# Two transformer blocks on one core: modulation blocks 0 to 10 summed in PE column groups, attention's divisions on DVE, value products one pair later, other load order

## The chip, the core and the metric

The kernel runs on one NeuronCore of a Trainium2 chip. Five engines work from queues of their own, in program order: PE (TensorE, matmuls), DVE (VectorE), ACT (ScalarE), POOL (GpSimd) and SP (SyncE, which here only issues DMAs). They wait for one another through semaphores that the program sets by hand. The metric is the device time of one execution in microseconds; lower is better. The median of three runs before the change is 988.04 us.

## What is computed

The input is a sequence of 256 tokens of width 1024. It goes through two blocks of a transformer, then through a third of another kind and a last norm. All weights are fp32.

```python
def first_block(x, c, ...):
    cond = silu(c)
    for i in range(2):
        mod = cond @ ada_w[i] + ada_b[i]                  # 1024 -> 6 * 1024
        sh1, sc1, g1, sh2, sc2, g2 = split(mod, 6)
        h = rmsnorm(x, norm1_g[i]) * (1 + sc1) + sh1
        y = sliding_window_sink_attention(h) if i == 0 else stick_breaking_attention(h)
        x = x + g1 * y
        h = rmsnorm(x, norm2_g[i]) * (1 + sc2) + sh2
        x = x + g2 * swiglu(h, w_gate[i], w_up[i], w_down[i])
    return x

def sliding_window_sink_attention(h):                     # 16 query heads of 64, 2 key heads
    ...                                                   # softmax over window and one sink column
    p = softmax(concat([s, sink])) [..., :-1]
    o = p @ v
    return o @ w_o
```

The third block takes its own `c_2` and `ada_w_2`. Its mixer is a spatial gate beside a causal convolution with a group norm, then an output projection `w_out` over both normed halves and a gated feed-forward of the same size. A last norm is shifted and scaled by `c_2 @ ada_f_w`.

The modulation vectors are 40 blocks of 512 outputs: blocks 0 to 11 are the first layer's, 12 to 23 the second's, 24 to 39 those of the third block and the last norm. Each block reads 1024 x 512 weights (2 MB).

## The kernel before

The activations lie transposed, [128 partitions, 8 tiles, 256 tokens]. Each weight matrix is streamed in units of 128 x 2048 fp32 (1 MB) into RAW, which has four slots. `high` on ACT rounds a unit to WH (fp32r), `low` on DVE takes the rest WL = RAW - WH, and PE makes three products for each tile (`three`: high by high, high by low, low by high; the lines 1739, 1740 and 1741 of the trace). A slot is loaded anew when its `low` is done (`unit_free`).

The modulation blocks are streamed through ADA, a buffer of one block with two halves; the first four blocks have places of their own (ADA, RAW twice, ADA3). `ada_sum` on DVE makes the product: eight instructions over [128, 512], each adding a weight tile times a column of COND to ACC (lines 1091 and 1094). For blocks 0 to 9 `ada_reduce` on PE then sums over the partitions, with four one-column matmuls, into AUX, and DVE adds the bias (`early_bias`, `ada_bias`) into MOD. Of block 3 the first four tiles go through PE alone (`ada_direct`). From block 10 on DVE transposes ACC in 32 x 32 blocks and sums, and four blocks are folded in one PE step (`fold_reduce`, line 1848).

The start: SP loads blocks 0 to 3 and x, and then the first projection's weights. PE turns x, ACT norms it. With MOD of blocks 0 to 3, `coefficients(0)` gives the scale (line 1153), ACT and DVE write the high and low parts of the scaled rows, and PE starts the key and value products.

The attention works on eight pairs of query heads, b = 0 to 7. For each, PE makes the scores (`sa_scores`), DVE the maxima (`sa_max`, lines 1448 to 1467), ACT the exponentials with their sums (`sa_exp`, lines 854 and 859), DVE the sum's reciprocal (`sa_divide`, lines 1475 and 1477), ACT the divisions (its own `sa_divide`, line 866), PE turns the weights (`sa_turn`, line 2099), ACT copies them (line 877), PE multiplies with the values (`sa_rows`, lines 2109 to 2113), ACT takes the high part (line 883) and DVE the low (`attn_low`, line 1483). The order is written out by hand, with scores, maxima and exponentials two pairs ahead; half a modulation block is summed on DVE in each pair.

From the second norm on, every norm starts in `first_group`: PE multiplies with unscaled rows UH and UL while the norm's root is still being made. ACT writes a row's high part and its square (lines 684 and 685), DVE the low part (`unscaled_low`, line 1168, whose operands X and UH lie in SBUF). The squares of tiles 0 to 3 are added on POOL (`square_sum`, lines 627 and 631, both operands in SBUF), and PE sums the others and that sum over the partitions (`norm_sums`, line 1894), between the second and the third row of the group. Norms 2 and 4 follow a feed-forward (`add_down`), norms 1, 3 and 5 an output projection (`add_out`), norm 6 is the last.

In the third block's output projection PE takes the groups' sums (`group_sums`), the group roots (`group_spread`), the sums of the second half's norm (`out_norm(1)`) and its root (`out_spread(1)`) between the tiles of units 0 and 1; unit 2 needs the rows normed with them, whose low parts are DVE's line 1690.

## Time and profile before

| | us |
|---|---|
| three runs, median (lowest to highest) | 988.04 (986.56 to 990.71) |
| the profiled execution, its own time | 988.17 |
| its span in the profile | 986.4 |
| PE busy | 940.4 (95%) |
| DVE busy | 797.1 (81%) |
| ACT busy | 496.2 (50%) |
| POOL busy | 34.0 (3%) |

The span is what the profile covers, from the first to the last instruction; the execution's own time is 1.8 us longer. PE is busy nearly throughout from 139 us to the end; before that it is not. The view by stretches tells, for each stretch, the busy time of each engine and the granted clock of PE (1.00 is 2.4 GHz, 0.50 is 1.2 GHz). In the timeline a row is a start, a duration, the engine, line, operation and tiles, a count of merged instructions and, in brackets, how long the engine had been idle and who released it. An fp32 matmul stands there as two records.

### The profile page before, as it was taken

Reading aid. Unit: us, or ns where it says so; the run is one execution under the profiler, and the core shown is the slowest. Engines: PE = TensorE matmul, PEld = TensorE weight load, DVE = VectorE, ACT = ScalarE, POOL = GpSimd, SP = SyncE. Lnnn points to the kernel's source line nnn. Section 1 sums busy time; section 2 is a strip of 40 time slices with the busy share of each in tenths; the row PEclk is TensorE's granted clock in tenths of the full one; section 3 lists DMA queues with packets and bytes.
Section 4 is the critical chain, followed back from the end, with each engine's and each line's share of the span. In section 5 each row is a group of like instructions: output and inputs, shape, how many; then the busy total and the mean of one; then the engine's idle time right before and its main releaser. Section 6 shows DMA issues by size and latency. Waiting matters only on the chain.

```text
span 986.4 us, 19404 instructions
## 1 busy us (share of the span) xinstructions
PE 940.4 (95%) x7627; PEld 900.5 (91%) x7627; DVE 797.1 (81%) x1155; ACT 496.2 (50%) x754; POOL 34.0 (3%) x52
## 2 busy tenths in 40 slices
PE   1898889999999999999999999999999999999998
PEld 1796569999999999988999999999988999999997
DVE  6885986999859989787699995999995599985832
ACT  2734955554433367565655443336665555443432
POOL 0400000000000010000000000003000000000001
PEclk9797869999999999999999999999999999999999
DMA  9990586499929997565159992998784349992911
GB/s 319 375 338 36 163 263 226 159 323 317 320 74 373 372 339 258 206 223 183 45 164 309 320 323 79 366 373 272 257 211 147 112 154 304 332 311 93 368 58 64
DMA packets 147473, 234.99 MB, mean 238 GB/s; under 512 B 6746, under 2 KB 78082, under 8 KB 147410
## 3 DMA queue, kind: packets, MB, share of 16 engines
q1 hardware_dynamic: 145328, 230.88, 68.4%
q0 software_dynamic: 1408, 2.62, 1.0%
q10 hardware_dynamic: 674, 0.63, 0.3%
q8 instruction: 42, 0.69, 0.3%
q14 instruction: 21, 0.17, 0.0%
HBM read 230.79 MB, written 1.05 MB: 235 GB/s over the span
## 4 chain that ended last, share of the span: by engine, by line
PE 81%; DVE 10%; DMA 3%; issue 2%; SPq 1%; ACT 1%; DVEq 0%; ACTq 0%
PE M L1739 20%; PE M L1740 19%; PE M L1741 19%; DVE ACC L1094 5%; DMA ADA<-in_ada_w 3%; PE AUX L1894 2%; DVE WL L1068 2%; PE M L1757 1%; PE M L1759 1%; PE M L1763 1%; PE AUX L2327 1%; PE AUX L1806 1%; PE AUX L1807 1%; PE M L1811 1%; PE AUX L1811 1%
## 5 line engine op out<-in xcount | busy, mean ns | idle before, releaser
L1739 PE MATMUL M<-XH,WH 128*128 128x256 f32 x1264 | 363.2, 287 | 4.8 <-DVE XL L1690 2.2
L664 ACT ACTIVATE WH<-RAW 128x2048 fp32r<-128x2048 f32 x135 | 257.1, 1913 | 219.7 <-DMA RAW<-in_w_down 69.9
L1740 PE MATMUL M<-XL,WH 128*128 128x256 f32 x1264 | 359.3, 284 | 0.0
L1741 PE MATMUL M<-XH,WL 128*128 128x256 f32 x1264 | 359.2, 284 | 0.0
L1068 DVE TENSOR_TENSOR WL<-RAW,WH 128x2048 fp32r<-128x2048 f32 x135 | 307.4, 2285 | 40.1 <-ACT WH L664 39.8
L1739 PEld LDWEIGHTS M<-XH,WH 128*128 128x128 f32 x1264 | 244.4, 193 | 7.2 <-issue 6.6
L1740 PEld LDWEIGHTS M<-XL,WH 128*128 128x128 f32 x1264 | 244.4, 193 | 0.3
L1741 PEld LDWEIGHTS M<-XH,WL 128*128 128x128 f32 x1264 | 244.2, 193 | 0.0
L1094 DVE SCALAR_TENSOR_TENSOR ACC<-ADA,COND,ACC 128x512 f32<-128x512 f32 x262 | 196.8, 751 | 9.1 <-DMA ADA<-in_ada_w 0.2
L1739 PE MATMUL M<-MH,WH 128*128 (+1 forms) x528 | 150.6, 285 | 1.3 <-DVE WL L1068 0.6
L1740 PE MATMUL M<-ML,WH 128*128 (+1 forms) x528 | 149.4, 283 | 0.0
L1741 PE MATMUL M<-MH,WL 128*128 (+1 forms) x528 | 149.4, 283 | 0.0
L1739 PEld LDWEIGHTS M<-MH,WH 128*128 128x128 f32 x528 | 101.2, 192 | 3.2 <-issue 3.1
L1740 PEld LDWEIGHTS M<-ML,WH 128*128 128x128 f32 x528 | 101.3, 192 | 0.0
L1741 PEld LDWEIGHTS M<-MH,WL 128*128 128x128 f32 x528 | 101.3, 192 | 0.0
L713 ACT ACTIVATE MH<-TMP 128x256 f32 (+1 forms) x66 | 25.1, 417 | 54.1 <-DVE TMP L1214 46.7
L1139 DVE SCALAR_TENSOR_TENSOR X<-M,MOD,X 128x256 f32<-128x256 f32 x48 | 20.5, 477 | 16.3 <-PE M L1741 16.3
L1858 PEld LDWEIGHTS AUX<-CONST,ACC 128*128 128x128 f32 x72 | 11.6, 246 | 23.0 <-DVE ACC L1094 23.0
L1858 PE MATMUL AUX<-CONST,ACC 128*128 128x1 f32 x72 | 12.1, 289 | 21.3 <-DVE ACC L1094 21.3
L627 POOL TENSOR_TENSOR SQS<-TMP 128x256 f32<-128x256 f32 x6 | 4.7, 781 | 723.0 <-ACT TMP L685 720.9
L1127 DVE TENSOR_TENSOR MOD<-AUX,VC 128x16 f32<-128x16 f32 (+1 forms) x8 | 1.4, 172 | 34.5 <-PE AUX L1848 34.5
L707 ACT ACTIVATE TMP<-M 128x256 f32<-128x256 f32 x60 | 19.3, 373 | 18.1 <-PE M L1741 18.1
(321 smaller groups left out, 1312.2 us busy)
## 6 DMA issues: line engine op xcount, KB each, us to landing
ADA<-in_ada_w SPq DMA_DIRECT2D x68, 1024.0 KB, 5.6
RAW<-in_w_gate SPq DMA_DIRECT2D x44, 512.0 KB, 6.1
RAW<-in_w_up SPq DMA_DIRECT2D x44, 512.0 KB, 7.4
RAW<-in_w_down SPq DMA_DIRECT2D x44, 512.0 KB, 8.0
RAW<-in_w_ffn_in SPq DMA_DIRECT2D x44, 512.0 KB, 6.8
RAW<-in_wqkv_b SPq DMA_DIRECT2D x24, 512.0 KB, 5.0
RAW<-in_w_ffn_out SPq DMA_DIRECT2D x22, 512.0 KB, 6.7
RAW<-in_w_in SPq DMA_DIRECT2D x16, 512.0 KB, 6.6
```

The source lines that it names most:

```text
L664: act.activation(WH[:, s, :], RAW[:, s, :], ACT.Copy).then_inc(h_ready, 1)
L707: act.activation(TMP[:, 2 * g + n, :], M[:, 4 * g + n, :], ACT.Silu).then_inc(silu_ready, 1)
L713: act.activation(MHF[:, bass.ds((i * 4 + 2 * g + n) * T, T)], TMP[:, 4 + 2 * g + n, :], ACT.Copy).then_inc(midh_ready, 1)
L1068: dve.tensor_tensor(WL[:, s, :], RAW[:, s, :], WH[:, s, :], ALU.subtract).then_inc(l_ready, 1)
L1094: dve.scalar_tensor_tensor(out=acc, in0=w, scalar=scale, in1=acc, op0=ALU.mult, op1=ALU.add).then_inc(a_chain, 1)
L1139: dve.scalar_tensor_tensor(out=X[:, j, :], in0=M[:, j, :], scalar=mod(layer, chunk, j), in1=X[:, j, :], op0=ALU.mult, op1=ALU.add).then_in ...
L1739: pe.matmul(out_ap, wh, xh, start=start, stop=False, skip_group_check=True)
L1740: pe.matmul(out_ap, wh, xl, start=False, stop=False, skip_group_check=True)
L1741: return pe.matmul(out_ap, wl, xh, start=False, stop=stop, skip_group_check=True)
L1811: mm = pe.matmul(FIRST[m], WH[:, s, cols], UL[:, kt, :], start=False, stop=kt == KT - 1, skip_group_check=True)
L1858: mm = pe.matmul(AUX[:, 6, at + j:at + j + 1], ACC[:, acc_slot(b), j * P:(j + 1) * P], cc(C_ONE), start=True, stop=True)
L1894: mm = pe.matmul(sums[:, n * m:n * m + n], squares[:, m * P:(m + 1) * P], columns, start=first and m == 0, stop=last, skip_group_check=True)
```

## The change

- Modulation blocks 0 to 10 are no longer summed on DVE. `ada_rows` on PE multiplies each weight tile, as the moving operand of 512 columns, with a column of COND that is broadcast to 32 columns; tile kt goes to column group kt mod 4, so that the four groups write four partial sums to the 32-partition bands of SUMS (AUX 6 and 7). `ada_turn` on DVE transposes SUMS and copies 16 columns into PART, and the blocks are folded as the later ones are: 0 to 3, 4 to 7, 8 and 9, then 10 to 13 and so on.
- On PE the blocks stand at the start, after units 2 and 3 of the first projection, before the first scores, after the second, and in pairs 1, 3 and 5.
- The divisions of the attention are four DVE instructions right behind the reciprocal. In a pair PE makes the scores first, then turns the weights, and multiplies the values of the pair before; ACT and DVE take the high and low part a pair later too.
- Loads: the rows of c go through ACT's queue; the larger part of the constants is loaded after the first rounding of the key and value weights; the loads of `wo_a` alternate with those of modulation blocks 5 to 8, and the loads of blocks up to 11 wait for PE's sums and not for DVE's.
- Norms: POOL adds the squares of five tiles instead of four, and PE has one less to sum.
- Output projection of the third block: ACT squares the centred rows straight from AUX, before `high` of unit 3, and DVE copies them after that; `group_sums` and `group_spread` stand one tile earlier, `out_norm(1)` after the first tile of unit 1 instead of the third, and `out_spread(1)` before its last tile.

On PE, one pair of the attention before (pair 2: weights turned, scores of pair 4, a reduction, value products; PR holds the softmax weights, PT the turned ones, VA the values):

```order
L2099 MATMUL AUX<-CONST,PR 128x128 x6
L2085 MATMUL M<-KS,QA 128x128
L2085 MATMUL M<-QA 128x128
L2087 MATMUL M<-KS,QA 128x256
L2087 MATMUL M<-QA 128x256
L2089 MATMUL M<-MASKA,IDB 128x384 x2
L1858 MATMUL AUX<-CONST,ACC 128x1 x4
L2109 MATMUL AUX<-PT,VA 64x128 x2
L2111 MATMUL AUX<-PT,VA 64x128 x2
L2113 MATMUL AUX<-PT,VA 64x128 x2
```

And after, pair 3, which carries a whole modulation block (line 1853):

```order
L2067 MATMUL M<-KS,QA 128x128
L2067 MATMUL M<-QA 128x128
L2069 MATMUL M<-KS,QA 128x256
L2069 MATMUL M<-QA 128x256
L2071 MATMUL M<-MASKA,IDB 128x384 x2
L2081 MATMUL AUX<-CONST,PR 128x128 x6
L2091 MATMUL AUX<-PT,VA 64x128 x2
L2093 MATMUL AUX<-PT,VA 64x128 x2
L2095 MATMUL AUX<-PT,VA 64x128 x2
L1853 MATMUL AUX<-ADA,COND 32x512 x8
```

The scores moved ahead of the turning, and eight matmuls over 512 columns took the place of four of one column.

On DVE, one pair of the attention before (reciprocal, maxima, half a block's sum, low part):

```order
L1475 TENSOR_TENSOR SM<-RS_SUM,SM 128x4
L1477 RECIPROCAL SM<-SM 128x4
L1448 TENSOR_REDUCE SM<-M 128x2 x2
L1462 TENSOR_TENSOR SM<-SM,QRS 128x4
L1464 SCALAR_TENSOR_TENSOR SM<-SM,NSINK 128x4
L1467 TENSOR_TENSOR SM<-SINK,SM 128x4
L1120 TENSOR_TENSOR MOD<-AUX,VC 128x4
L1091 TENSOR_SCALAR ACC<-ADA,COND 128x512
L1094 SCALAR_TENSOR_TENSOR ACC<-ADA,COND,ACC 128x512 x3
L1483 TENSOR_TENSOR XL<-AUX,XH 128x256
```

And after, in pair 3, from the reciprocal on:

```order
L1459 RECIPROCAL SM<-SM 128x4
L1463 TENSOR_SCALAR PR<-PR,SM 128x128
L1463 TENSOR_SCALAR PR<-PR,SM 128x256
L1463 TENSOR_SCALAR PR<-PR,SM 128x128
L1463 TENSOR_SCALAR PR<-PR,SM 128x256
L1432 TENSOR_REDUCE SM<-M 128x2 x2
L1446 TENSOR_TENSOR SM<-SM,QRS 128x4
L1448 SCALAR_TENSOR_TENSOR SM<-SM,NSINK 128x4
L1451 TENSOR_TENSOR SM<-SINK,SM 128x4
L1470 TENSOR_TENSOR XL<-AUX,XH 128x256
L1104 STREAM_TRANSPOSE ACC<-AUX 128x512
L1106 COPY PART<-ACC 128x16
```

The four divisions now stand between the reciprocal and the maxima of the next pair, and the half block's sum is gone, with a transpose and a copy in three of the eight pairs.

The diff, cut to its core:

```diff
-FOLDED = 10
-FOLDS = [range(b, min(b + 4, 40)) for b in range(FOLDED, 40, 4)]
+ON_PE = 11
+EARLY_FOLDS = [range(0, 4), range(4, 8), range(8, 10)]
+FOLDS = EARLY_FOLDS + [range(b, min(b + 4, 40)) for b in range(10, 40, 4)]
...
                     if b == len(EARLY):
-                        sp.wait_ge(a_chain, 4 * h + 4)
+                        sp.wait_ge(a_rows, h + 1)
+                    elif b <= ON_PE:
+                        sp.wait_ge(a_rows, 2 * (b - 1) + h + 1)
                     else:
                         sp.wait_ge(a_chain, summed(b - 1, 4 * h + 4) + 8 * i)
                     sp.dma_start(ADA[:, h, :, :], src[:, 4 * h:4 * h + 4, bass.ds(col, 512)]).then_inc(a_landed[h], 16)
...
-            for k in range(3):
+            for k in range(4):
                 load_square(U0["wo_a"], k, wo_a_src, 512 * (k // 2))
-            ada_block(5)
-            load_square(U0["wo_a"], 3, wo_a_src, 512)
-            for b in range(6, 11):
+                ada_block(5 + k)
+            for b in range(9, 11):
                 ada_block(b)
...
-                for j in range(2, 4):
+                for j in range(2, 5):
                     pool.wait_ge(sq_ready, KT * n + j + 1)
-                    pool.wait_ge(sq_sum, 3 * (n - 1) + j - 1)
+                    pool.wait_ge(sq_sum, 4 * (n - 1) + j - 1)
                     pool.tensor_tensor(SQS[:, :], SQS[:, :], TMP[:, j, :], ALU.add).then_inc(sq_sum, 1)
...
+            act.dma_start(CONST[:, KEPT_EARLY:K_W], a["kept"][:, KEPT_EARLY:K_W]).then_inc(rest_in, 16)
...
-            def sa_divide(b):
-                act.wait_ge(sa_r, b + 1)
-                p = b % 2
-                for e in range(2):
-                    for blk, lo, hi in ((0, 0, P), (1, P, 3 * P)):
-                        act.activation(PR[:, p, e, lo:hi], PR[:, p, e, lo:hi], ACT.Copy,
-                                       scale=SM[:, p, 5, 2 * e + blk:2 * e + blk + 1]).then_inc(sa_pn, 1)
+            def attn_high(b):
+                act.wait_ge(sa_o, b + 1)
+                act.activation(XH[:, b, :], AUX[:, 4, :], ACT.Copy).then_inc(hh_ready, 1)
             sa_exp(0)
-            sa_divide(0)
...
-                if b + 1 < 8:
-                    sa_divide(b + 1)
+                if b > 0:
+                    attn_high(b - 1)
                 if b + 2 < 8:
                     sa_exp(b + 2)
-                act.wait_ge(sa_o, b + 1)
-                act.activation(XH[:, b, :], AUX[:, 4, :], ACT.Copy).then_inc(hh_ready, 1)
+            attn_high(7)
...
+            for j in range(4):
+                act.wait_ge(gn_c, j // 2 + 1)
+                act.activation(TMP[:, j, :], AUX[:, j, :], ACT.Square).then_inc(gn_sq, 1)
             high(U0["w_out"], 3)
-            for j in range(4):
-                act.wait_ge(gn_copied, j + 1)
-                act.activation(TMP[:, j, :], CV[:, j, :], ACT.Square).then_inc(gn_sq, 1)
             act.wait_ge(gn_var, 1)
...
+            def ada_turn(b):
+                turned = ACC[:, b % 2, :]
+                if b >= 2:
+                    dve.wait_ge(part_ready, b - 1)
+                dve.wait_ge(a_rows, 2 * b + 2)
+                dve.transpose(turned, SUMS).then_inc(acc_turned, 1)
+                dve.wait_ge(acc_turned, b + 1)
+                dve.tensor_copy(PART[:, part_at(b):part_at(b) + 16], turned.rearrange("p (x r) -> p x r", r=32)[:, :, 0]).then_inc(part_ready, 1)
...
+            ada_turn(0)
             dve.wait_ge(ang_s, 2)
             dve.tensor_scalar(COS[:, :], COS[:, :], cc(C_ROPE), cc(C_KEEP), ALU.mult, ALU.add).then_inc(trig_ready, 1)
-            ada_sum(3, 0, rows=range(4, 8))
+            ada_turn(1)
+            root(0)
+            ada_turn(2)
+            ada_turn(3)
...
+            fold_bias(0)
+            coefficients(0)
             kv_low(0, kv_high, kv_low_ready)
-            early_bias()
-            coefficients(0)
             dve.wait_ge(t_ready, KT)
             dve.wait_ge(coef_ready, 1)
...
-                    dve.wait_ge(sa_pn, 4 * b - 4)
                 dve.tensor_tensor(SM[:, p, 4, :], RS_SUM[:, p, :], SM[:, p, 3, :], ALU.add).then_inc(sa_t, 1)
                 dve.wait_ge(sa_t, b + 1)
                 dve.reciprocal(SM[:, p, 5, :], SM[:, p, 4, :]).then_inc(sa_r, 1)
+                dve.wait_ge(sa_r, b + 1)
+                for e in range(2):
+                    for blk, lo, hi in ((0, 0, P), (1, P, 3 * P)):
+                        dve.tensor_scalar(PR[:, p, e, lo:hi], PR[:, p, e, lo:hi], SM[:, p, 5, 2 * e + blk:2 * e + blk + 1], None,
+                                          ALU.mult).then_inc(sa_pn, 1)
...
             qa_group(2)
+            ada_turn(6)
             sa_divide(0)
             sa_max(1)
+            ada_turn(7)
             for b in range(8):
                 if b + 1 < 8:
                     sa_divide(b + 1)
...
                     qa_recip(2)
                 if b + 2 < 8:
                     sa_max(b + 2)
-                if b % 2 == 0 and b > 0:
-                    ada_bias(5 + b // 2)
-                half = KT // 2 * (b % 2)
-                ada_sum(6 + b // 2, 0, rows=range(half, half + KT // 2))
-                attn_low(1, b)
-            low(U0["wo_a"], 1)
-            ada_bias(9)
-            low(U0["wo_a"], 2)
-            ada_sum(10, 0)
-            low(U0["wo_a"], 3)
+                if b > 0:
+                    attn_low(1, b - 1)
+                if b in (0, 4):
+                    fold_bias(1 + b // 4)
+                elif b in (1, 3, 5):
+                    ada_turn(8 + b // 2)
+            attn_low(1, 7)
+            for k in range(1, 4):
+                low(U0["wo_a"], k)
             add_out("wo_a", 0, 0)
...
-            def ada_reduce(b):
-                pe.wait_ge(a_chain, summed(b, KT))
-                if b > 3:
-                    pe.wait_ge(mod_ready, b)
-                at = 4 * b if b < 3 else 0
-                for j in range(4):
-                    mm = pe.matmul(AUX[:, 6, at + j:at + j + 1], ACC[:, acc_slot(b), j * P:(j + 1) * P], cc(C_ONE), start=True, stop=True)
-                mm.then_inc(acc_red, 1)
+            def ada_rows(b, h):
+                if b < len(EARLY):
+                    pe.wait_ge(early_landed[b][h], 16)
+                else:
+                    pe.wait_ge(a_landed[h], 16 * (b + 1 - len(EARLY)))
+                if h == 0 and b > 0:
+                    pe.wait_ge(acc_turned, b)
+                    if b in [fold[0] for fold in FOLDS]:
+                        pe.wait_ge(mod_ready, b)
+                w = EARLY[b if b < len(EARLY) else 0]
+                for kt in range(4 * h, 4 * h + 4):
+                    c = slice(32 * (kt % 4), 32 * (kt % 4) + 32)
+                    mm = pe.matmul(SUMS[c, :], COND[:, kt:kt + 1].to_broadcast([P, 32]), w[:, kt, :], start=h == 0, stop=h == 1,
+                                   skip_group_check=True)
+                mm.then_inc(a_rows, 1)
...
             def norm_sums(n):
-                for j in range(4, 6):
-                    mean_square(n, j)
-                pe.wait_ge(sq_sum, 3 * n)
+                mean_square(n, 5)
+                pe.wait_ge(sq_sum, 4 * n)
                 token_means(AUX[:, 0, 0:2], SQS, ONES[:, 0:1], False, False)
...
-            ada_reduce(0)
+            pe.wait_ge(cond_ready, 1)
+            ada_block(0)
+            pe.wait_ge(early_rows_in, 16 * row_dmas(EARLY_ROWS))
+            turn_rows(EARLY_ROWS)
+            ada_block(1)
             pe.wait_ge(x_in, 16)
             for j in range(KT):
                 for m in range(2):
                     mm = pe.transpose(M[:, j, m * P:(m + 1) * P], XTOK[:, m, j * P:(j + 1) * P], IDENT)
                 if j % 2 == 1:
                     mm.then_inc(x_turned, 1)
-            ada_reduce(1)
...
+            ada_rows(2, 1)
+            ada_block(3)
+            fold_reduce(0)
...
+            ada_block(7)
             for b in range(8):
-                sa_turn(b)
                 if b + 2 < 8:
                     sa_scores(b + 2)
-                if b % 2 == 0 and b > 0:
-                    ada_reduce(5 + b // 2)
-                sa_rows(b)
-            ada_reduce(9)
+                sa_turn(b)
+                if b > 0:
+                    sa_rows(b - 1)
+                if b in (0, 4):
+                    fold_reduce(1 + b // 4)
+                elif b in (1, 3, 5):
+                    ada_block(8 + b // 2)
+            sa_rows(7)
             group(U0["wo_a"], 0, 0, 0, 1)
...
-            unit(base, 0, 0, sets[0], range(0, 4), operand, True, False, between=[lambda: None, group_sums, group_spread])
+            unit(base, 0, 0, sets[0], range(0, 4), operand, True, False, between=[group_sums, group_spread, lambda: None])
             pe.wait_ge(ug_ready, 4)
-            unit(base, 1, 0, sets[1], range(0, 4), operand, True, False, between=[lambda: None, lambda: None, lambda: out_norm(1)])
-            out_spread(1)
+            unit(base, 1, 0, sets[1], range(0, 4), operand, True, False, between=[lambda: out_norm(1), lambda: None, lambda: out_spread(1)])
...
-            mean_square(6, 4)
             for j in range(4):
                 last_turn(j)
             mean_square(6, 5)
```

## Rows read from the trace of the kernel before

**Rows 1.** The page: the span.

```profile
span 986.4 us, 19404 instructions
```

**Rows 2.** By stretches: PE, PEld, DVE, ACT, POOL busy us, granted clock, DMA.

```profile
95.00:139.00 44.00, 34.59 (x234) 23.32 (x234) 37.45 (x94) 36.91 (x121) 0.00 (x0) 0.73 0.52 169
...
190.00:430.00 240.00, 239.44 (x1959) 233.87 (x1958) 210.29 (x264) 117.34 (x145) 4.10 (x3) 1.00 0.80 278
...
770.00:774.00 4.00, 3.63 (x18) 3.66 (x19) 1.23 (x4) 3.98 (x4) 0.00 (x0) 0.57 0.02 4
```

**Rows 3.** Timeline of the start, DVE and PE: start, duration, instruction, idle before.

```profile
32.78 0.48 DVE L1091 TENSOR_SCALAR ACC<-ADA,COND 128x512 f32<-128x512 f32 x1 [1.77 <-DMA ADA<-in_ada_w]
...
38.67 0.16 DVE L1114 TENSOR_TENSOR MOD<-AUX,VC 128x4 f32<-128x4 f32 x1 [1.16 <-PE AUX L2001]
...
40.40 0.55 PE L1739 MATMUL M<-XH,WH 128*128 128x256 f32 x1 [1.77 <-DVE XL L1366]
```

**Rows 4.** Prices: page group, timeline of PE's column groups, lines' durations (ns).

```profile
L1094 DVE SCALAR_TENSOR_TENSOR ACC<-ADA,COND,ACC 128x512 f32<-128x512 f32 x262 | 196.8, 751 | 9.1 <-DMA ADA<-in_ada_w 0.2
...
734.98 5.39 PE L2327 MATMUL AUX<-ADA,DG 128*32 128x256 f32 x96
...
L1103 DVE STREAM_TRANSPOSE ACC<-ACC x30: 711/712/715, 149.4 to 921.3; 128x512 f32<-128x512 f32 x30
```

**Rows 5.** Timeline of the attention: ACT, DVE and PE, pairs 0 to 7.

```profile
92.03 0.46 ACT L854 ACTIVATE PR<-M,SM,QRS 128x128 f32<-128x128 f32 x1
...
104.25 0.15 DVE L1475 TENSOR_TENSOR SM<-RS_SUM,SM 128x4 f32<-128x4 f32 x1
...
104.64 1.49 ACT L866 ACTIVATE PR<-PR,SM 128x128 f32<-128x128 f32 x4 [0.37 <-DVE SM L1477]
104.66 0.95 DVE L1448 TENSOR_REDUCE SM<-M 128x2 f32<-128x256 f32 x2
...
106.05 0.46 ACT L854 ACTIVATE PR<-M,SM,QRS 128x128 f32<-128x128 f32 x1
...
108.02 0.20 ACT L859 ACTIVATE SM<-SM 128x4 f32<-128x4 f32 x1
...
126.38 0.44 ACT L854 ACTIVATE PR<-M,SM,QRS 128x128 f32<-128x128 f32 x1
...
129.55 1.87 PE L1858 MATMUL AUX<-CONST,ACC 128*128 128x1 f32 x8 [2.47 <-DVE ACC L1094]
...
137.79 1.87 PE L1858 MATMUL AUX<-CONST,ACC 128*128 128x1 f32 x8 [1.21 <-DVE ACC L1094]
```

**Rows 6.** Timeline: a DVE scaling of 256 columns by a column of scales.

```profile
7.37 0.35 DVE L1329 TENSOR_SCALAR ANG<-ANG,CONST 128x256 f32<-128x256 f32 x1
```

**Rows 7.** Timeline of the third block's output projection, PE.

```profile
767.59 0.60 PE L1902 MATMUL AUX<-CONST,RSTD 128*128 128x128 f32 x4
...
770.37 0.55 PE L1739 MATMUL M<-XH,WH 128*128 128x256 f32 x1 [2.17 <-DVE XL L1690]
```

**Rows 8.** Timeline of norm 2: DVE, POOL and PE.

```profile
362.06 1.27 DVE L1168 SCALAR_TENSOR_TENSOR UL<-X,COEF,UH 128x256 fp32r<-128x256 f32 x3
362.10 1.82 POOL L631 TENSOR_TENSOR SQS<-SQS,TMP 128x256 f32<-128x256 f32 x1
363.36 0.84 DVE L1168 SCALAR_TENSOR_TENSOR UL<-X,COEF,UH 128x256 fp32r<-128x256 f32 x1
364.12 2.28 DVE L1068 TENSOR_TENSOR WL<-RAW,WH 128x2048 fp32r<-128x2048 f32 x1
364.22 0.58 PE L1894 MATMUL AUX<-CONST,SQS 128*128 128x1 f32 x4
```

**Rows 9.** Timeline of norm 3: POOL, DVE and PE.

```profile
487.95 0.74 POOL L631 TENSOR_TENSOR SQS<-SQS,TMP 128x256 f32<-128x256 f32 x1
488.80 0.47 DVE L1168 SCALAR_TENSOR_TENSOR UL<-X,COEF,UH 128x256 fp32r<-128x256 f32 x1
490.34 0.58 PE L1894 MATMUL AUX<-CONST,SQS 128*128 128x1 f32 x4
```

151 lines of the change are left out of this document (56 added, 95 removed).

## The prediction, made before the changed kernel was run

> **What bounds the kernel now.** I read the page's span first [rows 1], then the view by stretches, in order of time [rows 2]. From 190 to 430 us PE is busy 239.4 of 240 us at full clock, and it stays so nearly to the end: there every microsecond of PE's work, and every wait of PE, goes straight into the time, and work taken off DVE brings nothing. Between 95 and 139 us, in the attention, it is otherwise: DVE is busy 37.5 of 44 us, ACT 36.9, PE 34.6 at a mean clock of 0.73. So the change's large edit, modulation off DVE, can pay only before 139 us, by letting PE reach the output projection earlier; behind that only edits of PE's own row count. The timelines of single stretches follow: the start [rows 3], the attention [rows 5], the one long wait of PE in the third block [rows 7], and the norms [rows 8, 9]. The sum is made against the profiled execution's own 988.17 us, its span and 1.8 us around it; the median of the runs, 988.04, is the same within 0.2.
>
> **The price of a block on PE.** DVE pays eight instructions of 0.75 us for a block, 6.0 us [rows 4], and PE a reduction of 1.87 at half clock [rows 5], about 1.0 at full. For the new form the nearest row is the convolution, which runs 128x32 matmuls in four column groups: 96 records in 5.39 us [rows 4] are 12 sets of four fp32 matmuls of 256 columns, 0.45 us a set, so the four groups do run side by side. At 512 columns a set is 0.9, a block 1.8 us; at half clock 3.6. DVE then has a transpose of 0.71 [rows 4] and a small copy, 0.9 together. PE pays more than before, DVE 5 us less a block.
>
> **The start.** The last weights of block 3 land at 32.78, the first modulation is added up at 38.67, and PE starts at 40.40 [rows 3]. After: half a block 0.9 to 1.8, transpose and copy 0.9, the fold some 0.5, bias 0.2, so 2.5 to 3.4 us behind the landing instead of 5.9. The landing comes up to 1.7 us earlier (SP begins without two issues; a third of a megabyte of constants follows later). But the first `low` of the key weights, 1.1 us, now stands behind the coefficients. That gives 2 to 4.5 us at the first product. Until the first exponential PE then pays 0.75 to 1.0 more for each of blocks 4 and 5 and 1.8 for block 6. I take a first exponential 1.4 us earlier, bounds 0 to 3.
>
> **The attention.** Before, the first exponential starts at 92.03 and the eighth at 126.38, 4.9 us a pair [rows 5]. What paces it after? The exponentials of a pair take 108.22 - 106.05 = 2.2 us; then DVE adds and inverts (104.25 to 104.64, 0.4), and from 104.66 to 106.05 it makes the next pair's maxima, 1.4 [rows 5]. The divisions, 1.49 on ACT [rows 5], today run beside these maxima. On DVE they stand ahead of them: two of 256 columns at 0.27 apart (0.35 less overlap, [rows 6]) and two of 128 at 0.20 to 0.27, 0.9 to 1.1 us. The new ring is 2.2 + 0.1 + 0.4 + 1.0 + 1.4 = 5.0 us: exponentials, reciprocal, divisions, the next maxima, the next exponentials. It has taken the place of the old pace: ACT and DVE get idle time and the pair stays at 5 us. Seven pairs are 35.0 instead of 34.35, a loss of 0.7. The order on PE (scores first) keeps this ring free of PE for about 3 us of delay: PE was busy 34.6 us for eight pairs at a clock of 0.73 [rows 2], 4.3 a pair, which is some 3.2 at full clock and 6 at half; a block adds 1.8 or 3.6. At full clock that is less than the ring or level with it, at half clock more; I allow 1.3 us for stretches at half clock.
>
> The end of the attention is shorter. Before, PE waited 2.47 us for a DVE sum and reduced it for 1.87 ahead of pair 6's value products, and again 1.21 and 1.87 ahead of the projection [rows 5]. Both go. The second is 3.1 us on the path whole; of the first I count 1.4, since the turning of the last weights is next behind it. Value products a pair later cost nothing there: the last pair's products wait for the low part of the pair before as they do now. Together 4.5. The attention and what is before it: 1.4 - 0.7 - 1.3 + 4.5 = **3.9 us** earlier at the projection, bounds 0 to 7. The `high` and `low` of `wo_a` unit 1 follow the attention by 4.6 us and lie under unit 0, which PE works on for 5.8 us or more; the first gate weights now load before it, since SP no longer stands behind block 9's sum. Behind 139 us PE is full, so the 3.9 us stay.
>
> **The third block's output projection.** PE waits 2.17 us for the normed rows, which come 2.8 us after the root was spread at 767.59 [rows 7], and then has a mean clock of 0.57 for 4 us [rows 2]: some 3.3 us at 1.2 GHz, which costs 1.5. After: squares before `high`, sums one tile earlier, `out_norm(1)` two tiles earlier and the spread ahead of the last tile, some 2.3 us earlier in PE's own work. About 0.7 us of wait is left, after which the trace shows no fall of the clock. Gain 1.5 + 1.4 = **2.9 us**, bounds 1 to 3.6.
>
> **The norms.** One square less on PE is 0.4 us in each of six norms, if POOL's added tile is there in time. In norms 1 and 6 it is (in norm 1 DVE idles then; in norm 6 its other operand is in PSUM): 0.8. In norm 2 it is not. POOL's last add began at 362.10, just after DVE's first `unscaled_low`, and took 1.82 us instead of the 0.74 of norm 3 [rows 8, 9]: it came through only where DVE had a gap, before the instruction at 363.36, which in turn took 0.84 instead of 0.48. It ended at 363.92, and PE took the sum at 364.22 [rows 8]. So a POOL add waits while DVE runs instructions with two SBUF operands back to back. The fifth tile's add would start at 364.06, while the last `unscaled_low` ends and `low` follows at 364.12 without a gap, also with two SBUF operands (RAW and WH), until 366.3. I take it that POOL waits for that too: its add ends at 367.05, PE takes the sum at 367.1, 2.9 us later than today, with some 3 us idle. After 2.17 us of idling the clock cost 1.5 us above; I put 1.6 here. Norm 4's records lie the same. Cost 2 x (2.9 + 1.6) = **9.0 us**; lower bound, if POOL gets in at 364.06, 0.7 a norm. The Trainium skill, page SBUF — State Buffer, section Who interferes with whom, has the rule: a DVE instruction with two SBUF inputs contends with a GpSimd one that reads SBUF, and whoever is first holds the shared port for the whole instruction. The trace agrees for the `unscaled_low` (1.82 against 0.74); for `low` no row shows it.
>
> In norms 3 and 5 POOL's fifth add would start at 488.83, within 0.03 us of a DVE instruction at 488.80 [rows 9] that is followed by three more and a `low`. It could go first (gain 0.4), slip in before the fourth, or wait to 492.6. I take nothing for both, between +0.4 gained and 3.2 lost each.
>
> **Sum.** 988.2 - 3.9 - 2.9 - 0.8 + 9.0 = 989.6 us: the gains are eaten by one moved addition.
>
> **Rivals.**
> R1, POOL gets in: it takes its turn ahead of `low`, and each of norms 2 and 4 costs 0.7 while 3 and 5 give 0.4 each: 988.2 - 3.9 - 2.9 - 0.8 - 0.8 + 1.4 = 981.2. For it: the start is only 0.06 us from DVE's, and a pending instruction may be served between two others. Against it: in the run of three that starts at 362.06 it was not, at two boundaries [rows 8].
> R2, POOL is shut out in all four norms: norms 3 and 5 cost 3.2 + 1.6 each, since `low` there follows the four at 0.4 apart, from 490.4 to 492.6, and PE's sum is today at 490.34 [rows 9]: 999.2. It is on the slower side, and decides at whether POOL or DVE asks first at 488.8.
> R3, PE paces the attention: if it stays at half clock (0.73 was the mean, [rows 2]) a pair needs 6 us and one with a block 9, and the gain of 3.9 turns into 0 to 3 lost: 995 with the norms as forecast, 987 with R1. Against it: PE will idle less.
> R4, the column groups don't overlap for 512 columns (four times the price, 5.4 us more for each of eleven blocks): over 1020; the convolution speaks against it.
>
> **How the numbers follow.** Forecast 0.40 (987 to 993), R1 0.32 (978 to 984), R2 0.13, R3 0.11, others 0.04. The range leaves out the low edge of R1 and the high edge of R2: 979 to 998. A measurement can tell 0.5% here, 4.9 us: faster than 983.1 is most of R1 and little of the forecast, 0.31; slower than 993 is R2, most of R3 and the upper edge of the forecast, 0.30; the rest 0.39.
>
> **What would show it.** In the profile after: sums of a block of about 0.9 us a half on PE; exponentials 5.0 us apart; the first product of the output projection near 135.6; POOL's fifth add of norms 2 and 4 lasting some 3 us, with a PE idle of about 3 us before the sum of POOL's squares and a lower clock behind it; the wait of unit 2 of `w_out` under 1 us. I am wrong if POOL's fifth add takes 0.74 us there, or if the exponentials come every 4 us.

## The result and the profile after

The changed kernel takes 979.58 us in the median (978.55 to 981.21, four runs), the kernel before 989.38 on the same chip (986.56 to 993.56). The ratio is 0.990, with a 95% interval of 0.987 to 0.993. The kernel before scatters by some 10 us from run to run (984.1 to 994.3 over all runs below), so kernels from different chips are compared by their ratios only, and differences of 2 us or less are read in the traces. The prediction was wrong: it forecast 989.6 us, no gain at all, and the time lies 10 us below that, at the lowest edge of its whole range (979 to 998). The time is near that of rival R1 (981.2), but, as the next sections show, by another sum.

The page of the profiled execution (its own time is 978.55), span and first section:

```profile
span 976.8 us, 19474 instructions
PE 937.0 (96%) x7691; PEld 878.8 (90%) x7691; DVE 756.9 (77%) x1118; ACT 484.8 (50%) x722; POOL 39.4 (4%) x58
```

DVE has lost 40 us of work and the span 9.6 us [rows 1]. By stretches (busy us of PE, PEld, DVE, ACT and POOL, granted clock, DMA share, GB/s):

```profile
96.00:128.00 32.00, 23.85 (x235) 13.42 (x233) 22.28 (x85) 20.51 (x75) 0.00 (x0) 1.00 0.63 217
131.50:150.00 18.50, 18.50 (x142) 18.50 (x141) 11.06 (x10) 12.62 (x13) 0.00 (x0) 0.90 0.73 241
190.00:430.00 240.00, 238.64 (x1926) 231.75 (x1925) 208.03 (x261) 118.55 (x150) 4.82 (x4) 0.99 0.79 276
```

The same stretch of the attention in the kernel before:

```profile
96.00:128.00 32.00, 26.59 (x190) 16.43 (x188) 27.84 (x77) 29.10 (x103) 0.00 (x0) 0.81 0.49 157
```

From 96 us on, in the attention's loop, PE now runs at full clock where it had 0.81 (the 0.73 of [rows 2] takes in the start and the end of the attention, which are at half clock in both kernels), and has 8 of 32 us free. From 190 to 430 us, where it was always busy at full clock before [rows 2], it now idles for 1.4 us and the clock falls once. The timeline of PE at the start and in the attention (start, duration, instruction, idle before it and who ended that):

```profile
33.15 0.26 PE L1837 MATMUL AUX<-PART,CONST 128*32 128x16 f32 x8 [1.16 <-DVE PART L1106]
36.22 0.47 PE L1727 MATMUL M<-XH,WH 128*128 128x256 f32 x1 [2.81 <-DVE XL L1353]
...
109.93 1.92 PE L1853 MATMUL AUX<-ADA,COND 128*32 128x512 f32 x16
...
131.50 0.58 PE L1745 MATMUL M<-XH,WH 128*128 128x256 f32 x1
```

and the projection's first product in the kernel before:

```profile
139.52 0.56 PE L1757 MATMUL M<-XH,WH 128*128 128x256 f32 x1
```

ACT and DVE around pair 3, and ACT's first and last exponentials:

```profile
88.24 0.46 ACT L858 ACTIVATE PR<-M,SM,QRS 128x128 f32<-128x128 f32 x1
...
98.36 0.46 ACT L858 ACTIVATE PR<-M,SM,QRS 128x128 f32<-128x128 f32 x1 [1.24 <-DVE SM L1448]
...
100.63 0.16 DVE L1457 TENSOR_TENSOR SM<-RS_SUM,SM 128x4 f32<-128x4 f32 x1 [2.02 <-ACT SM L863]
100.83 0.18 DVE L1459 RECIPROCAL SM<-SM 128x4 f32<-128x4 f32 x1
101.04 1.01 DVE L1463 TENSOR_SCALAR PR<-PR,SM 128x128 f32<-128x128 f32 x4
...
102.13 0.95 DVE L1432 TENSOR_REDUCE SM<-M 128x2 f32<-128x256 f32 x2
...
103.51 0.46 ACT L858 ACTIVATE PR<-M,SM,QRS 128x128 f32<-128x128 f32 x1 [1.95 <-DVE SM L1448]
...
123.74 0.46 ACT L858 ACTIVATE PR<-M,SM,QRS 128x128 f32<-128x128 f32 x1 [1.85 <-DVE SM L1448]
```

The first product is at 36.22 (40.40 before [rows 3]), the first exponential at 88.24 (92.03 [rows 5]), the projection's first product at 131.50, where it was at 139.52. These are single traces, and the starts scatter: two more traces of the changed kernel (a_again, a_again_b, below) have the projection at 133.30 and 132.43, two more with the start of the kernel before (b_pool_five, b_out_between) at 141.59 and 143.03. The means of the three are 132.4 and 141.4, 9.0 us apart. A whole block costs PE 1.92 us at full clock (estimate: 1.8). From pair 3 on ACT waits 1.85 to 1.95 us in each pair for DVE, which goes through reciprocal, divisions and maxima one behind the other. Norm 2, one of the two norms in which the prediction put its 9 us (POOL, DVE, PE; the groups of [rows 8]):

```profile
352.50 1.81 POOL L633 TENSOR_TENSOR SQS<-SQS,TMP 128x256 f32<-128x256 f32 x1
353.76 0.83 DVE L1156 SCALAR_TENSOR_TENSOR UL<-X,COEF,UH 128x256 fp32r<-128x256 f32 x1
354.45 0.73 POOL L633 TENSOR_TENSOR SQS<-SQS,TMP 128x256 f32<-128x256 f32 x1
354.52 2.81 DVE L1067 TENSOR_TENSOR WL<-RAW,WH 128x2048 fp32r<-128x2048 f32 x1
355.24 0.61 PE L1886 MATMUL AUX<-CONST,SQS 128*128 128x1 f32 x4 [0.93 <-POOL SQS L633]
```

POOL's added addition starts 0.07 us ahead of `low`, takes 0.73 us, and it is `low` that pays: 2.81 instead of 2.28 us [rows 8]. PE waits 0.93 us. In the output projection of the third block, the waits of PE from 755 to 768 us (engine, what waited and for whom: us, times, longest):

```profile
PE M L1727 <- DVE XL L1678: 0.7, 1, 0.7
```

The wait of 0.7 us was 2.17 before [rows 7]. Put together, by the start of POOL's first addition in each norm (159.01, 359.53, 486.18, 681.02, 782.96 and 975.13 us before; 150.00, 349.93, 478.79, 673.54, 773.27 and 965.93 after):

| stretch | forecast | measured |
|---|---|---|
| to the output projection | -3.9 | -8.0 |
| projection to norm 1 | 0 | -1.0 |
| norm 1 to 2 | -0.4 | -0.6 |
| norm 2 to 3 | +4.5 | +2.2 |
| norm 3 to 4 | 0 | -0.1 |
| norm 4 to 5 (with `w_out`) | +1.6 | -2.2 |
| norm 5 to 6 | 0 | +0.5 |
| norm 6 to the end | -0.4 | -0.4 |
| sum | +1.4 | -9.6 |

Two questions follow: what POOL's addition costs and why, and what in the attention gives 8 us.

### The profile page after: what moved, and what is told of

Its sections match the earlier page's. It is cut to its first block, busy times and chain, and to the rows that moved or that the text cites. A ratio compares the mean times of both kernels' runs of the same rounds, so it can differ in the third digit from the quotient of the medians.

```text
span 976.8 us, 19474 instructions
## 1 busy us (share of the span) xinstructions
PE 937.0 (96%) x7691; PEld 878.8 (90%) x7691; DVE 756.9 (77%) x1118; ACT 484.8 (50%) x722; POOL 39.4 (4%) x58
## 4 chain that ended last, share of the span: by engine, by line
PE 83%; DVE 8%; ACT 3%; DMA 2%; issue 2%; POOL 1%; SPq 0%; DVEq 0%; ACTq 0%; POOLq 0%
PE M L1727 21%; PE M L1728 20%; PE M L1729 20%; DVE WL L1067 2%; DMA TMP<-in_x 2%; PE AUX L1886 2%; PE AUX L1853 1%; PE M L1745 1%; PE M L1747 1%; PE M L1751 1%; PE AUX L2314 1%; ACT PR L858 1%; POOL SQS L633 1%; PE AUX L1794 1%; PE AUX L1799 1%
## 5 line engine op out<-in xcount | busy, mean ns | idle before, releaser
L1727 PE MATMUL M<-XH,WH 128*128 128x256 f32 x1264 | 361.9, 286 | 3.8 <-DVE XL L1353 2.8
L1084 DVE SCALAR_TENSOR_TENSOR ACC<-ADA,COND,ACC 128x512 f32<-128x512 f32 x203 | 152.5, 751 | 7.0 <-DMA ADA<-in_ada_f_w 0.3
L1745 PE MATMUL M<-XH,WH 128*128 128x256 f32 x96 | 25.3, 294 | 0.0
L1211 DVE TENSOR_TENSOR ML<-TMP,MH 128x256 f32 (+1 forms) x66 | 24.8, 418 | 0.5 <-ACT MH L717 0.5
```

The lines of the kernel that those rows point to most:

```text
L1084: dve.scalar_tensor_tensor(out=acc, in0=w, scalar=scale, in1=acc, op0=ALU.mult, op1=ALU.add).then_inc(a_chain, 1)
L1211: dve.tensor_tensor(MLF[:, at], TMP[:, 4 + 2 * g + n, :], MHF[:, at], ALU.subtract).then_inc(mid_ready, 1)
L1727: pe.matmul(out_ap, wh, xh, start=start, stop=False, skip_group_check=True)
L1745: pe.matmul(M[:, tau, :], WH[:, s, cols], xh, start=first and q == 0 and tau % 2 == 0, stop=False, skip_group_check=True)
```

## Experiments on GpSimd's addition and the clock

The first theory A was that the addition is worth little where it is in time and costs where it is late; the prediction had said that it is shut out by `low`. A and B are named anew in each expectation.

**Taken back.** In all norms, and then in norms 2 and 4 alone:

```diff
-                for j in range(2, 5):
+                for j in range(2, 4):
```

> The changed kernel with GpSimd's fifth square addition taken back in all six norms (three tiles added up behind the first pair's, PE takes four squares itself again). Theory A (the late addition costs in norms 2 and 4, where PE waited 0.93 us for it and the granted clock then fell to 0.67 for 4 us, and gives about 0.1 us of PE time in the others): no wait of PE for GpSimd's sum in norm 2, clock 1.00 behind it, the stretch from norm 2 to norm 3 back from 128.9 to 126.7 us; in all 1.5 to 3 us faster than the changed kernel, 976.5 to 978. Theory B (the addition is worth its 0.4 us of PE in every norm, and the lost clock behind norm 2 is chance): 2 us slower, 981.5, and the stretch from norm 2 to norm 3 stays at 128.5 or more.

Measured: 976.32 us, ratio 0.9885 (0.9867 to 0.9903), an interval that overlaps with that of the changed kernel (0.987 to 0.993). From norm 2 to 3 it takes 126.64 us, and PE has no wait there: theory A in this stretch. But two falls of the clock now stand behind norms 1 and 5 (201.80 and 193.51 us to the next norm, instead of 199.93 and 192.66), and of the 4.5 us saved behind norms 2 and 4 one or two are left.

```diff
-                for j in range(2, 5):
+                for j in range(2, 5 if n not in (2, 4) else 4):
```

> The changed kernel with the fifth addition taken back in norms 2 and 4 alone. Theory A: as with all six taken back in norms 2 and 4, and 0.1 to 0.4 us kept in each of norms 1 and 6: 976 to 977.5. Theory B: 0.8 us slower than the changed kernel, 980.4.

Measured: 978.84, ratio 0.9913 (0.9897 to 0.993): nearer to theory B, though again inside the interval of the changed kernel. PE does not wait in norm 2, and the clock fell all the same; the 8 us that begin 4 us behind the norm's start, and one of them alone:

```profile
355.18:363.18 8.00, 8.00 (x58) 8.00 (x57) 4.81 (x8) 3.85 (x7) 0.38 (x1) 0.79 0.85 300
358.00:359.00 1.00, 1.00 (x7) 1.00 (x6) 0.12 (x2) 0.00 (x0) 0.00 (x0) 0.50 0.61 227
```

PE was busy all 8 us, at a mean clock of 0.79 and for a time at 0.50, and the way to norm 3 took 128.31 us. So a fall needs no wait of PE; theory A's cause of the falls was too simple.

**Alone in the kernel before.** The same line the other way round, 4 to 5.

> The kernel before with GpSimd's fifth square addition alone. Theory A (the addition gets in ahead of the long subtraction, in 0.7 to 1.0 us; PE waits some 0.9 us for it in norms 2 and 4 and saves 0.4 in norms 1 and 6): within 1.5 us of before, 986 to 988.5. Theory B, my prediction (the addition is shut out until the subtraction is over): 3 us for that addition in norms 2 and 4, 8 to 9 us slower, 996. Theory C (0.4 us saved in every norm): 985.

Measured: 989.39 against 989.04, ratio 1.0001 (0.9977 to 1.0026). Theory A. The added addition costs nothing that can be measured (the interval is some 2.5 us to either side), where the prediction had it at 8.2 (9.0 less 0.8).

**The changed kernel again.**

> The changed kernel itself, once more, beside the others of this group. The question is where the granted clock falls behind 150 us, each fall costing some 1.7 us: in the first trace in norms 2 and 4. Theory A (the wait of 0.93 us for GpSimd's sum brings the fall): the same two norms again, and nowhere else before the tail. Theory B (any norm's run of one-column matmuls may bring it, and which one does so is chance): at least one fall in another norm, or a different number of them; the wait of 0.93 us stays where it was. Time 977 to 979.5 either way, since two falls are usual in all traces so far.

Measured: 979.54, ratio 0.9897 (0.984 to 0.9953), and the falls stand behind norms 2 and 4 again. That looks like theory A, but over all traces of this document the falls are a matter of counts. From norm 2 to norm 3 the kernels with a wait of 0.9 us took 128.86 to 128.95 us in eight traces and 130.41 in one, with a fall each, and 127.29 and 127.30 in two, without one. The kernels without the wait took 126.64 to 126.66 in five traces and 128.31 in one, with the fall shown above. So **the wait itself costs 0.65 us and a fall 1.6**, and a fall came in nine of eleven traces with the wait and in one of six without. Kernels without the additions had falls behind norm 1 or 5 instead, in four of five traces.

**One addition more.** Whether `low` holds POOL at all was open, since the fifth tile's addition came ahead of it in every trace. With a sixth tile one comes due behind `low`:

```diff
-                for j in range(2, 5):
+                for j in range(2, 6):
```

> The changed kernel with one more tile of squares on GpSimd (a sixth), so that an addition comes due in norms 2 and 4 while the vector engine's long subtraction stands ready to start or runs. Theory A (the two engines take turns: whichever is asked first runs its whole instruction, and the other goes next, so the subtraction starts 0.5 us late behind the fifth addition and the sixth then waits for its whole 2.3 us): sixth addition over at about 358.4 in a trace whose norm 2 starts at 349.9, PE waits 3.5 to 4.3 us there, 5 to 7 us slower than the changed kernel. Theory B (an addition is never held for long by the subtraction, the fifth was not at its start only by luck): sixth addition 0.7 to 1.0 us, PE waits 1.7 us, 1 to 2 us slower.

Measured: 988.1 us, ratio 1.0002 (0.998 to 1.0025), 8.5 us slower than the changed kernel of the same chip (979.61). Theory A, and somewhat dearer. POOL and DVE in norm 2:

```profile
355.92 0.73 POOL L633 TENSOR_TENSOR SQS<-SQS,TMP 128x256 f32<-128x256 f32 x1
355.99 2.81 DVE L1067 TENSOR_TENSOR WL<-RAW,WH 128x2048 fp32r<-128x2048 f32 x1
356.79 2.59 POOL L633 TENSOR_TENSOR SQS<-SQS,TMP 128x256 f32<-128x256 f32 x1
```

and the wait of PE there, from 351 to 361 us:

```profile
PE AUX L1886 <- POOL SQS L633: 3.7, 1, 3.7
```

The fifth addition comes first and `low` waits for it; the sixth asks 0.8 us behind `low`'s start and is held until `low` ends at 358.80, then takes its 0.6. Norm 2 to norm 3 took 132.45 us. This is what the prediction had described for the fifth: the mechanism exists and was put one addition too early. The Trainium skill, page SBUF — State Buffer, section Who interferes with whom, calls the port pair that DVE and GpSimd share an exclusive lock and says that the order of issue decides who blocks. The trace agrees in both directions (2.81 instead of 2.28 us for DVE, 2.59 instead of 0.73 for POOL).

## Experiments on the attention and the start

**The modulation and its load order alone.** Divisions on ACT, products in the same pair with PE's old order, four tiles on POOL, `w_out` as before (the edits below, together):

> The changed kernel with all but the modulation blocks and the load order undone: divisions on ScalarE, value products in the same pair and PE's order of the pair as before, four tiles on GpSimd, the output projection as before. Theory A (nearly all of the gain ahead of the output projection is the modulation: no wait of PE for the vector engine's sums at the start, in the units and at the two ends of the attention, and a vector engine free of 3 us a pair): first exponential near 88.3, projection at 131 to 133, 978 to 981.5. Theory B (the later value products and the divisions carry the attention's part, the modulation gives only the 3.8 us of the start): projection at 135 to 136.5, 983 to 984.5.

Measured: 975.35 us, ratio 0.987 (0.9806 to 0.9935), better than either theory said and at least as good as the whole change (979.54 on this chip; the intervals overlap). First exponential 88.42, projection 129.53. The modulation on PE, with its load order, carries the gain; the rest of the change adds nothing to it that can be measured. No run takes these two apart. The load order may have a share at the start: SP issues the first load of block 3 at 11.06 us, where it was 14.28, and the products of block 3 at 30.06 wait for DVE's transpose of the block before and no longer for a DMA.

**The divisions.** ACT's `sa_divide` put back, its call after the copies of each pair:

```diff
+            def sa_divide(b):
+                act.wait_ge(sa_r, b + 1)
+                p = b % 2
+                for e in range(2):
+                    for blk, lo, hi in ((0, 0, P), (1, P, 3 * P)):
+                        act.activation(PR[:, p, e, lo:hi], PR[:, p, e, lo:hi], ACT.Copy,
+                                       scale=SM[:, p, 5, 2 * e + blk:2 * e + blk + 1]).then_inc(sa_pn, 1)
```

> The changed kernel with attention's divisions back on ScalarE, where they run beside the vector engine's maxima. Theory A (ring): 2.2 + 0.4 + 1.5 + 0.2 = 4.2 to 4.5 us a pair instead of 5.06, so 4 to 6 us earlier at the projection, 974 to 976: moving the divisions was a loss. Theory B (the divisions on ScalarE hold up its copies and exponentials, as in the kernel before, where a pair took 4.9): 4.8 to 5.1 us a pair and 978.5 to 980.5.

Measured: exponentials 4.45 us apart (88.86 to 120.01), as the ring says, projection at 129.26; the time of 977.5 (0.9893, 0.9868 to 0.9917), which lies between the ranges of the two theories, did not show it, since behind norm 2 a longer fall of the clock made it 130.41 us to norm 3. Once more on one chip with its rivals:

> The changed kernel once more, as the measure for the two that follow on the same chip. Falls of the clock behind 150 us: by theory A of its first repetition in norms 2 and 4 again. 0.99 of the time of before.

Measured: 979.61, ratio 0.9915 (0.9888 to 0.9943). In norm 4 POOL's additions were shorter this time (3.00 us the three, instead of 4.26) and PE waited only 0.2 us for them (norm 4 to 5: 97.34 us), as also in two further traces (a_max_first and a_ring_double, 3.01 and 3.02 us); behind norm 2 the clock fell again. The expectation held at norm 2 alone.

> Divisions back on ScalarE, once more beside the changed kernel on one chip, with more rounds. Theory A (the shorter ring, 4.45 against 5.06 us in the traces, is worth the 2 to 3 us that the projection is earlier): 2 to 3.5 us faster than the changed kernel of this group. Theory B (behind the attention the clock takes it back, as the first medians suggest): within 1 us.

Measured: 974.58, ratio 0.9864 (0.9838 to 0.989), 5 us faster than the changed kernel beside it. Theory A in direction, and more than its 2 to 3.5; the two traced executions are 2.3 apart (span 973.7 against 976.0), since neither is the median of its kernel (975.49 and 977.77 us). The pairs were 4.45 apart but for one of 5.8. **Moving the divisions to DVE was a loss**: some 2 us at the projection in the traces, 0.5 and 5 us in the two comparisons of times.

**The order on DVE.** In the loop over the pairs:

```diff
-                if b + 1 < 8:
-                    sa_divide(b + 1)
                 if b == 1:
                     qa_recip(2)
                 if b + 2 < 8:
                     sa_max(b + 2)
+                if b + 1 < 8:
+                    sa_divide(b + 1)
```

> The changed kernel with the maxima of a pair issued on the vector engine ahead of the reciprocal and divisions of the pair before it. Theory A (the pace of 5.06 us a pair is a ring: exponentials 2.2, reciprocal 0.4, divisions 1.0, maxima 1.4, each behind the other; with the maxima running beside the exponentials it opens, and the next limit is PE with some 3.2 us a pair and 1.9 for a block): exponentials 3.8 to 4.4 us apart, the first product of the output projection 5 to 7 us earlier, 973 to 975. Theory B (PE, its scores and its blocks, paces the attention, and the ring only seems to fit): exponentials stay within 0.3 us of 5.06, and the time within 1 us of the changed kernel.

Measured: 971.13, ratio 0.9835 (0.9816 to 0.9854). The pairs come 4.28 us apart (90.79 to 120.78) and the projection at 128.35. Theory A by the pace; the time is 2 us better than its range, the projection 3.2 us earlier and not 5 to 7, since in this trace the first exponential was 2.5 us later. The waits between 96 and 128 us name what may limit next, the turned weights, the blocks' DMA and PE:

```profile
ACT PT L877 <- PE AUX L2081: 5.8, 5, 2.4
PEld AUX L1853 <- DMA ADA<-in_ada_w: 4.9, 3, 2.1
DVE ACC L1104 <- PE AUX L1853: 3.6, 4, 1.4
PEld M L2067 <- ACT PR L858: 3.3, 3, 1.6
ACT PR L858 <- DVE SM L1448: 3.2, 2, 2.9
```

In the changed kernel the wait of the exponentials for the maxima was the largest, from 99 to 128 us:

```profile
ACT PR L858 <- DVE SM L1448: 9.3, 5, 1.9
DVE SM L1457 <- ACT SM L863: 8.4, 6, 2.0
PEld AUX L2091 <- DVE XL L1470: 5.4, 5, 1.5
```

> Maxima ahead of the divisions, once more beside the changed kernel on one chip, with more rounds: 6 to 8 us faster than the changed kernel of this group by theory A (the ring was the limit, PE and the weights' DMA are next); under 4 us if the first measurement was lucky.

Measured: 969.29, ratio 0.9808 (0.978 to 0.9835), 10.3 us faster than the changed kernel on its chip: more than expected. The projection starts at 126.42, 6.0 us earlier than in a_again_b. This version beats both kernels.

**Both together.** Maxima first and four tiles on POOL:

> The changed kernel with the maxima ahead of the divisions, and GpSimd's fifth addition taken back. Theory A: the two gains seen apart add up, 6.4 and 1: 969.5 to 972, no wait of PE for GpSimd's sum, the stretch from norm 2 to norm 3 at 126.7. Theory B (behind the attention the clock gives back what the additions cost, as its falls then come in norms 1 and 5): 971.5 to 974.

Measured: 971.22, ratio 0.9842 (0.9797 to 0.9887). The stretch from norm 2 to 3 is 126.65, but there were falls behind norms 1 and 5 (201.69 and 193.56 us), as theory B has it. The median lies in theory A's range, the ratio shows no gain over the maxima alone (0.9835 and 0.9808), and the interval holds both theories.

**The value products.** Back in the same pair, divisions left on DVE:

```diff
-                if b + 2 < 8:
-                    sa_scores(b + 2)
                 sa_turn(b)
-                if b > 0:
-                    sa_rows(b - 1)
+                if b + 2 < 8:
+                    sa_scores(b + 2)
...
+                sa_rows(b)
```

> The changed kernel with value products, their high and low parts and PE's order within a pair as in the kernel before; divisions stay on the vector engine. Theory A (the later products buy nothing: the pace is the ring of exponentials, divisions and maxima, and at the end the last pair's products wait for the low part either way, as the modulation alone had 7.8 us from the last exponential to the projection and the changed kernel 7.8 to 8.7): exponentials 5.0 to 5.1 apart, projection within 0.7 us of 131.5 to 133.3, time 978 to 980.5. Theory B (they hide the way from turned weights over ScalarE's copy to the products, 1 us a pair): 1.5 to 4 us slower, 981 to 983.5.

Measured: 983.04, ratio 0.9955 (0.9935 to 0.9975), in the range of theory B. Theory A is wrong. The pairs are 5.6 us apart from the third on, and DVE shows why:

```profile
107.51 0.42 DVE L1468 TENSOR_TENSOR XL<-AUX,XH 128x256 fp32r<-128x256 f32 x1 [1.48 <-ACT XH L868]
107.85 0.15 DVE L1455 TENSOR_TENSOR SM<-RS_SUM,SM 128x4 f32<-128x4 f32 x1
108.03 0.18 DVE L1457 RECIPROCAL SM<-SM 128x4 f32<-128x4 f32 x1
```

The low part of the same pair waits for ACT's high part, which stands behind the exponentials, and the next pair's reciprocal, divisions and maxima are queued behind it: `low` enters the ring, +0.5 us a pair. A pair later it is out of the ring. With the divisions on ACT the later products gave nothing that shows: 41.1 us from first exponential to projection with the modulation and load order alone, 40.4 and 41.7 in the two traces with products a pair later. So this edit mends what moving the divisions would cost; theory B's hidden latency is not what it bought.

**PE's cover.** Two extra passes of the first half's matmuls, first in blocks 8 to 10, then in blocks 4 and 5:

```diff
-                for kt in range(4 * h, 4 * h + 4):
+                again = 2 if h == 0 and b in (8, 9, 10) else 0
+                for kt in [4 * h + q % 4 for q in range(4 + 4 * again)]:
```

> The changed kernel with two more passes of the first half's four matmuls in blocks 8, 9 and 10, which lie inside the attention's loop: 5.8 us more on PE at full clock, same result. Theory A (the ring has 1.9 us a pair without a block free on PE, so a block of 3.8 us is nearly hidden): exponentials stay 5.06 apart but for the pairs with a block, 0 to 2 us in all, 979 to 981.5. Theory B (PE paces the loop): 5 to 6 us in all, 984.5 to 985.5.

Measured: 976.99, ratio 0.9883 (0.985 to 0.9917), no slower than the changed kernel; exponentials of the first and eighth pair from 90.66 to 126.23, 35.57 us as against 35.50. All 5.8 us are hidden. Theory A: in the loop a block on PE is free.

> The changed kernel with two more passes of the first half's four matmuls in blocks 4 and 5, which lie in the unit stage ahead of the attention: 2 x 1.92 = 3.84 us more on PE at full clock, same result. Theory A (PE paces that stage after the change, at full clock, and each block costs its 1.9 us there): first exponential 3.3 to 4.3 us later, 982.5 to 984. Theory B (the stage has slack, which is why four blocks on PE cost so little ahead of the first exponential): under 1.5 us later.

Measured: 981.94, ratio 0.9946 (0.9927 to 0.9964), 4 to 5 parts in a thousand above the changed kernel: theory A by the time. From the first product to the first exponential it took 55.2 us, against 52.0 and 52.2 in the traces of the changed kernel and of the modulation alone, like it without a fall of the clock in that stage: 3.1 more, of 3.84. The fourth trace without a fall there (a_pool_mixed) has 52.4; the eleven other traces with the new start have one between 64 and 72 us, and there it is 53.0 to 54.3.

**The output projection.** Its part of the change alone in the kernel before, ACT's earlier squares and DVE's later copies with it:

```diff
-            unit(base, 0, 0, sets[0], range(0, 4), operand, True, False, between=[lambda: None, group_sums, group_spread])
+            unit(base, 0, 0, sets[0], range(0, 4), operand, True, False, between=[group_sums, group_spread, lambda: None])
...
-            unit(base, 1, 0, sets[1], range(0, 4), operand, True, False, between=[lambda: None, lambda: None, lambda: out_norm(1)])
-            out_spread(1)
+            unit(base, 1, 0, sets[1], range(0, 4), operand, True, False, between=[lambda: out_norm(1), lambda: None, lambda: out_spread(1)])
```

> The kernel before with the edit of the third block's output projection alone (squares from PSUM ahead of the last high part, sums a tile earlier, the second norm two tiles earlier). Theory A, as predicted: the wait of 2.17 us falls under 1 us and the clock stays at full behind it, 2.5 to 3 us faster: 984.5. Theory B (the stretch from norm 4 to norm 5 became shorter in the changed kernel by other things): 986.5 to 988.

Measured: 988.06 against 989.04, ratio 0.9992 (0.9962 to 1.0021): the time cannot tell the theories apart. The wait is 0.7 us, as predicted. Norm 4 to 5 took 97.45 us without a fall, and 98.90 in the modulation alone, where the wait is still 2.2 us. There the clock stayed full behind that wait:

```profile
757.00:763.00 6.00, 5.51 (x46) 5.54 (x47) 1.55 (x6) 5.35 (x5) 0.00 (x0) 1.00 0.00 0
```

In the trace of b_pool_five, too, the clock stayed at 1.00 behind a wait of 2.2 us. So the edit is worth 1.5 us, and the 1.4 that I added for the clock was a fall that happens to stand in the trace of before.

## Why the prediction was wrong, step by step

The change was forecast at +1.4 us and measured at -9.6. Of the 11.0 between them, 6.1 stand in the stretches from norm 2 to 3 and from norm 4 to 5, and 5.1 ahead of norm 1.

- **Norms 2 and 4, +9.0: wrong, the largest error.** The failed step is "I take it that POOL waits for that too". The prediction had both starts 0.06 us apart, 364.06 for POOL and 364.12 for `low`, POOL first, and then gave `low` the turn. POOL had it, in 11 of 11 traces of norm 2 (and in the one with six tiles). The row at 363.36, 0.84 instead of 0.48 us [rows 8], had already shown an addition served between two DVE instructions that stood back to back. The lower bound (0.7 a norm) was the right value without a fall: 0.65 measured. With the falls norm 2 cost 2.2. In norm 4 the trace of before already had one, so none was added there.
- **The first exponential, -1.4: mis-sized, -3.8 measured.** The 1.4 is not the sum of its own terms: a first product 2 to 4.5 us earlier, less 3.3 to 3.8 for blocks 4 to 6, gives from 1.2 earlier to 1.8 later (and the 2 to 4.5 is by its terms 1.4 to 4.0). The slip brought the forecast nearer to the measurement, by luck. Measured, the first product came 4.2 us earlier, in the repetitions 5.6 (and the first exponential 3.0 and 2.9). Not taken off the 3.3 to 3.8 were the reduction's own wait for DVE's sum, 1.1 us, which is gone, and a fall of the clock in the same stage, 1.7 us (the row below). That the fall is missing in the trace of the changed kernel is chance, since both repetitions have one there. In this trace it takes 0.4 us more from first product to first exponential, in the repetitions 2.7.

The kernel before, that stage by busy time and clock, columns as above:

```profile
68.00:76.00 8.00, 7.88 (x53) 7.53 (x52) 5.08 (x9) 3.46 (x6) 0.00 (x0) 0.79 1.03 373
```

- **Half clock in the loop, +1.3: wrong.** The clock was 1.00 from 96 us on, and the doubled blocks show that PE had more than 5 us to spare. **The ring, 5.0 us: right** (5.06, 35.5 us for seven pairs). The terms written down add up to 5.1, which would have been a loss of 1.35; measured is 1.15 (35.5 less 34.35), forecast was 0.7. That DVE's low part stays out of the ring was luck; the prediction never named it.
- **The end of the attention, -4.5: -5.4 measured** (13.1 to 7.8 us from last exponential to projection), and 1.0 us more of clock behind it.
- **`w_out`, -2.9:** 1.5 is real, the wait of 0.7 exact. The rest was a fall of the clock, and the trace of the changed kernel has one fewer there.
- **Norms 1 and 6, -0.8:** -0.6 and -0.4. Norms 3 and 5, 0: -0.1 and +0.5.

The rival R1 came out near in time, with a term of the same sign at the norms; but by its own sum the attention's gain was half of what it is. R2, R3 and R4 are refuted: norms 3 and 5 changed by -0.1 and +0.5 us, PE runs at full clock in the loop, and a block takes 1.92 us.

What stays open: what decides in which norm the clock falls, and how the gain ahead of the attention divides between the modulation's move to PE and the load order.

## What to carry to other kernels

When two engines ask for the same thing within 0.1 us of each other, follow the order that the trace's starts give; one more such instruction, behind the boundary, brought the price of 8.5 us. Work moved between engines in a loop has to be put at its place in the ring of waits: 1 us of divisions moved into the ring cost some 2 us in the traces, though DVE had idle time, while issuing the maxima ahead of them took 6 to 10 us off. And a fall of PE's clock seen once in one trace is not a price of the wait in front of it: look at several traces before adding it to a sum.

## What was not expected of the hardware

- An addition on POOL of 0.73 us that starts 0.07 us ahead of DVE's subtraction delays it by 0.53 us; one that asks 0.8 us behind its start is held for 2.0 us.
- Falls of the granted clock to the lower level, 1.2 GHz, for 1.6 us of loss each, came behind norms with no idle time of PE at all (clock 0.79 over 8 busy us), and did not come behind an idle time of 2.2 us in two traces of three.
- The whole of 5.8 us of extra matmuls was hidden in the attention's loop: seven pairs took 35.57 us instead of 35.50.
